# Dilated attention: query blocks without keys behind them taken two in a step, and the forget gates' sums spread through memory instead of by matmuls

## The chip, the cores and the metric

The kernel is one program on one core of a Trainium2 chip. The metric is the device time of one execution in microseconds (us); less is better.

## The reference, cut to what matters

Three transformer blocks follow each other. The change is in the attention of the second one: six heads of dilated attention (three branches, mixed by their softmax sums) and six heads of forgetting attention, 1024 tokens, heads of 64.

```python
def forgetting_attention(q, k, v, log_f):
    c = jnp.cumsum(log_f, axis=1)
    ...
        s = jnp.einsum('bqhd,bkhd->bhqk', qi, k) * scale
        s = s + jnp.transpose(ci, (0, 2, 1))[..., None] - c_k     # c_k: c of every key, for each head
        s = jnp.where(kpos[None, :] <= qpos[:, None], s, -jnp.inf)
        p = jax.nn.softmax(s, axis=-1)
...
DILATION_PAIRS = ((128, 1), (512, 4), (2048, 16))                 # window, dilation
def dilated_branch(q, k, v, window, dilation):
    blk = window // dilation                                      # 128 queries
    ...
    # keys of a query block: its own 128 and the 128 before them (with that dilation), if there are any
    s = jnp.einsum('bnqrhd,bnkrhd->bnrhqk', qs, kc) * (Dh ** -0.5)
    m = jnp.max(s, axis=-1, keepdims=True)
    e = jnp.exp(s - m)
    l = jnp.sum(e, axis=-1)
    num = jnp.einsum('bnrhqk,bnkrhd->bnqrhd', e, vc)
```

## The kernel before, in words

Everything before and after this stage is dense projections and MLPs on TensorE. The stage of interest lies between the last projection of the second block (`ka2`) and the first scores of forgetting attention.

The dilated part is cut into 72 units, `DUN = (branch, pair of heads, query block)`, 24 for each branch. A unit has 128 queries of two heads. `has_prev` says whether there are 128 keys behind its own 128: in branch 0 for 7 of 8 blocks, in branch 1 for 4 of 8, in branch 2 for none. Branches 1 and 2 read the queries and keys with a step of 4 and 8 elements (`dtok`); branch 0 reads them side by side.

Each unit passes through six operations on three engines, staggered over four steps of one loop:

- `dscores` (TensorE, L911): two heads' matmuls into one of two double banks `ps[0]`, `ps[1]`, 128 or 256 keys wide;
- `dmax` (VectorE, L2218): for each head, mask, negate, and keep the minimum, out of PSUM into `pd[n % 3]`;
- `dsoft` (ScalarE, L1544): exp in place with its sum, for each head;
- `dturn` (TensorE, L941), two steps behind the scores: 2 or 4 transposes of 128x128 into one half of `ps[2]`;
- `dcopy` (VectorE L1837, or ScalarE L1535 where `by_act` says so): that half into `qd_[n % 3]`, 256 or 512 columns;
- `dpv` (TensorE, L960), three steps behind: 2 or 4 matmuls with the values into `misc`. `dout` moves `misc` to `NUM` after every fourth unit (L1553 on ScalarE, L1837 on VectorE).

TensorE's order in step s is `dscores(s)`, `dturn(s-2)`, `dpv(s-3)`. VectorE's is `dmax(s)`, `dcopy(s-2)`, `dout(s-3)`; ScalarE's `dsoft(s-1)`, `dcopy(s-2)`, `dout(s-3)`.

Six times in that loop, after units 5, 17, 29, 41, 53 and 65, TensorE also makes `gate_sums(hd)` (L929): a matmul for each 512 columns, of `SEL` (a 6-row selector) with `CF` (the six heads' sums of the forget gates, 6 rows x 1024), which write row `hd` to all 128 partitions of the `ps` bank whose turn it is. ScalarE's `gate_out` (L1558) copies it with scale -1 to `CN[:, hd, :]`. The next user of that bank but one waits for this copy. The first `soft` of forgetting attention on VectorE (L2239) reads `CN`, and its scores (L975) come right behind the last dilated steps.

SyncE issues all DMAs (L2785) in program order: the weights of the next stage, `V4`, `SEL`, then, each behind its branch, the small stores `msc<-ML`, the load of `V16`, and `MN<-msc`.

A float32 matmul shows as two records, so x4 of L911 or x8 of L960 are two and four matmuls.

Of the kernel before, what the change touches and what calls it, by code (L numbers as in the profile page):

```python
# [16 lines left out]
P = 128  # L17
# [190 lines left out]
DSEQ = []  # L208
for _n in range(len(DUN)):
    DSEQ.append(("unit", _n))  # L210
    if _n % 12 == 5:
        DSEQ.append(("gate", _n // 12))

# [32 lines left out]
def build(nc, d, out):  # L246
    ctx = ExitStack()
    with ctx:
# [97 lines left out]
        SEL = at("SEL", RO, [6, 6, P])  # L346
# [50 lines left out]
        msc = nc.dram_tensor("msc", (S, 36), F, kind="Internal").ap()  # L397

# [44 lines left out]
        dnames = (["const", "meta", "mask", "wg", "sgl0", "sgl1", "vs", "sel", "v4", "v16", "b3", "out"]  # L443
# [22 lines left out]
        def dslot(n):  # L466

            return ps[DSEQ.index(("unit", n)) % 2]

# [14 lines left out]
        def by_act(n):  # L484

            br, t_, u = DUN[n]
            return has_prev(br, u) == 1 and u % 3 == 0
# [43 lines left out]
        def tensor(e):  # L531
# [369 lines left out]
            def dscores(n):  # L901

                br, t_, u = DUN[n]
                pv_ = has_prev(br, u)
                w = P * (1 + pv_)
                side_by(("unit", n))
                if n == 0:
                    q.wait_ge(*dv("kb2"))
                for hh in range(2):
                    r_ = slice(64 * hh, 64 * hh + 64)  # L910
                    i = e.matmul(dslot(n)[:, 512 * hh:512 * hh + w], dtok(QB[r_, t_, :], br, u, 0), dtok(KB[r_, t_, :], br, u, pv_), start=True, stop=True)  # L911
                i.then_inc(*pe.inc(f"ds{n}"))

            def side_by(x):

                i = DSEQ.index(x)
                if i > 1:
                    what, m = DSEQ[i - 2]
                    q.wait_ge(*(dv(f"dm{m}") if what == "unit" else ac(f"cn{m}")))
                elif held[i]:  # L920
                    q.wait_ge(*freed(held[i]))
# [10 lines left out]
            def dturn(n):  # L932
                br, t_, u = DUN[n]
                q.wait_ge(*ac(f"dp{n}"))
                if n > 1:
                    q.wait_ge(*at_of(f"dq{n - 2}"))
                elif held[2]:
                    q.wait_ge(*freed(held[2]))
                at_ = 512 * (n % 2)
                for j in range(2 * (1 + has_prev(br, u))):  # L940
                    i = e.transpose(ps[2][:, at_ + P * j:at_ + P * j + P], pd[n % 3][:, blk(j)], ident[:])  # L941
                i.then_inc(*pe.inc(f"dT{n}"))

            def dpv(n):

                br, t_, u = DUN[n]
                nb, g = 1 + has_prev(br, u), n // 8
                q.wait_ge(*at_of(f"dq{n}"))
# [7 lines left out]
                for j in range(nb):  # L956
                    v_ = (VB[:, (u - nb + 1 + j) % 8, :], V4[:, (4 * (u // 4 - nb + 1 + j) + u % 4) % 8, :], V16[:, u, :])[br]
                    for hh in range(2):
                        hd = 2 * t_ + hh
                        i = e.matmul(misc[64 * hh:64 * hh + 64, blk(u)], v_[:, 64 * hd:64 * hd + 64], qd_[n % 3][:, blk(nb * hh + j)], start=(j == 0), stop=(j == nb - 1))  # L960
                i.then_inc(*pe.inc(f"dpv{n}"))
# [18 lines left out]
            n = len(DUN)  # L980
            for s_i in range(n + 4):
                if s_i < n:
                    dscores(s_i)
                    if s_i % 12 == 5:
                        gate_sums(s_i // 12)
# [8 lines left out]
            def fturn(n):  # L994
# [3 lines left out]
                for hh in range(2):  # L998
                    if n:
                        q.wait_ge(*(dv if hh else ac)(f"fq{n - 1}"))  # L1000
                    else:
                        q.wait_ge(*at_of("dq70"))
                        q.wait_ge(*at_of("dq71"))
# [198 lines left out]
        def scalar(e):  # L1202
# [323 lines left out]
            def dcopy(n):  # L1526

                br, t_, u = DUN[n]
                if not by_act(n):
                    return  # L1530
                w = 2 * P * (1 + has_prev(br, u))
                q.wait_ge(*pe(f"dT{n}"))
                if n > 2:
                    q.wait_ge(*pe(f"dpv{n - 3}"))
                e.activation(qd_[n % 3][:, 0:w], ps[2][:, 512 * (n % 2):512 * (n % 2) + w], ACT.Copy).then_inc(*ac.inc(f"dq{n}"))  # L1535

            def dsoft(n):
                br, t_, u = DUN[n]
                w = P * (1 + has_prev(br, u))
                for hh in range(2):  # L1540
                    q.wait_ge(*dv(f"dm{n}" if hh else f"dm{n}a"))
                    p_ = pd[n % 3][:, w * hh:w * hh + w]
                    c_ = 2 * t_ + hh
                    i = e.activation(p_, p_, ACT.Exp, scale=-1.0, bias=ML[:, br, u, c_:c_ + 1], accum_out=ML[:, br, u, 6 + c_:7 + c_])  # L1544
                    i.then_inc(*ac.inc(f"dp{n}" if hh else f"dp{n}a"))

            def dout(n):

                br, t_, u = DUN[n]
                if u != 7:  # L1550
                    return
                q.wait_ge(*pe(f"dpv{n}"))
# [14 lines left out]
            n = len(DUN)  # L1567
            q.wait_ge(*pe("ka2"))
            for s_i in range(n + 4):
# [6 lines left out]
                if s_i < n and s_i % 12 == 6:  # L1576
                    gate_out(s_i // 12)
# [4 lines left out]
            def fcopy(n):  # L1582
# [3 lines left out]
                q.wait_ge(*(pe(f"fpv{n - 3}") if n > 2 else pe("dpv71")))  # L1586
# [240 lines left out]
        def vector(e):  # L1827
# [330 lines left out]
            log_sum("fa", T[1][0:6, :], T[0][0:6, :])  # L2158
# [40 lines left out]
            def dcopy(n):  # L2199
                br, t_, u = DUN[n]  # L2200
                if by_act(n):
                    return
                w = 2 * P * (1 + has_prev(br, u))
                q.wait_ge(*pe(f"dT{n}"))
                if n > 2:
                    q.wait_ge(*pe(f"dpv{n - 3}"))
                copy(qd_[n % 3][:, 0:w], ps[2][:, 512 * (n % 2):512 * (n % 2) + w], f"dq{n}")

            def dmax(n):

                br, t_, u = DUN[n]
                pv_ = has_prev(br, u)
                w = P * (1 + pv_)
                q.wait_ge(*pe(f"ds{n}"))
                q.wait_ge(*(pe(f"dT{n - 3}") if n > 2 else pe("ka2")))
                for hh in range(2):
                    c_ = 2 * t_ + hh
                    e.tensor_tensor_reduce(out=pd[n % 3][:, w * hh:w * hh + w], in0=dslot(n)[:, 512 * hh:512 * hh + w], in1=dmask(br, pv_), scale=-1.0, scalar=3.0e38, op0=ADD, op1=MIN, accum_out=ML[:, br, u, c_:c_ + 1]).then_inc(*dv.inc(f"dm{n}" if hh else f"dm{n}a"))  # L2218

            def dout(n):  # L2220
# [3 lines left out]
                q.wait_ge(*pe(f"dpv{n}"))  # L2224
                copy(dnum(br, t_, 0), v3(misc[:, 0:512], 4), f"nu{n // 8} 0")

            def soft(k, i_):
# [13 lines left out]
            n = len(DUN)  # L2241
# [11 lines left out]
            def fcopy(n):  # L2253
# [3 lines left out]
                q.wait_ge(*(pe(f"fpv{n - 3}") if n > 2 else pe("dpv71")))  # L2257
# [522 lines left out]
        def sync(e):  # L2780
# [324 lines left out]
```

## Time and profile before

| what | value |
|---|---|
| median of 3 runs | 3621.45 us (3615.03 to 3622.73) |
| profiled execution, its own time | 3618.45 us |
| its span, first to last instruction | 3616.3 us |
| TensorE busy (matmul) | 3517.2 us, 97% |
| VectorE, ScalarE busy | 1604.5 us, 1013.1 us |
| chain that ended last | TensorE 91%, VectorE 4%, ScalarE 2% |
| mean granted clock of TensorE | 0.975 |
| first scores L911 to first scores L975 | 1461.78 to 1625.58 us, 163.8 us |

The page gives times of one profiled execution. A view of it in order of time gives the start of a group of instructions, how long it lasted, its engine, line and operands, the number of records, and, in brackets, the idle time of the engine before it with what ended it. TensorE's durations overlap, since matmuls are pipelined: what a group costs there is the distance from its start to the start of the next group, not its duration. PEclk is the clock that TensorE was granted: 1.00 is 2.4 GHz and 0.50 is 1.2 GHz, its two levels; values between them are means of a stretch that has both.

### The profile page before, as it was taken

Reading aid. Unit: us, or ns where it says so; the run is one execution under the profiler, and the core shown is the slowest. Engines: PE = TensorE matmul, PEld = TensorE weight load, DVE = VectorE, ACT = ScalarE, POOL = GpSimd, SP = SyncE. Lnnn points to the kernel's source line nnn. Section 1 sums busy time; section 2 is a strip of 40 time slices with the busy share of each in tenths; the row PEclk is TensorE's granted clock in tenths of the full one; section 3 lists DMA queues with packets and bytes.
Section 4 is the critical chain, followed back from the end, with each engine's and each line's share of the span. In section 5 each row is a group of like instructions: output and inputs, shape, how many; then the busy total and the mean of one; then the engine's idle time right before and its main releaser. Section 6 shows DMA issues by size and latency. Waiting matters only on the chain.

```text
span 3616.3 us, 39495 instructions
## 1 busy us (share of the span) xinstructions
PE 3517.2 (97%) x17066; PEld 2827.0 (78%) x17066; DVE 1604.5 (44%) x1648; ACT 1013.1 (28%) x1458; POOL 1265.9 (35%) x647
## 2 busy tenths in 40 slices
PE   8999999999999999998999999999998999999997
PEld 6887888888888788655688888888887778888886
DVE  4654343333333485445545445444635351222224
ACT  5423221111112411544423222222322333222222
POOL 3113335444444322001223343443534353333333
PEclk9999999999999999969999999999999999999998
DMA  2112212222222211100111232231311121111113
GB/s 107 39 55 81 101 53 88 88 88 88 93 90 79 77 64 47 48 2 3 59 47 54 70 98 63 95 99 62 106 41 35 41 79 50 50 47 50 48 49 119
DMA packets 88569, 239.80 MB, mean 66 GB/s; under 512 B 13238, under 2 KB 20166, under 8 KB 88268
## 3 DMA queue, kind: packets, MB, share of 16 engines
q1 hardware_dynamic: 88396, 237.28, 20.2%
q8 instruction: 134, 2.20, 0.3%
q14 instruction: 39, 0.32, 0.0%
HBM read 219.27 MB, written 17.97 MB: 66 GB/s over the span
## 4 chain that ended last, share of the span: by engine, by line
PE 91%; DVE 4%; ACT 2%; POOL 2%; DMA 1%; issue 0%; SPq 0%; DVEq 0%; ACTq 0%
PE ps L576 27%; PE ps L577 26%; PE ps L579 26%; PE ps L911 2%; PE ps L941 1%; PE ps L960 1%; PE ps L975 1%; POOL wlo L2580 1%; PE ps L746 1%; DVE T L1831 1%; PE ps L1022 1%; PE ps L1006 1%; POOL GL L2586 1%; PE ps L604 0%; PE ps L606 0%; PE ps L1036 0%
## 5 line engine op out<-in xcount | busy, mean ns | idle before, releaser
L2580 POOL TENSOR_TENSOR wlo<-raw,whi 128x1024 fp32r<-128x1024 f32 (+3 forms) x367 | 697.3, 1900 | 1672.0 <-ACT whi L1217 1671.9
L576 PE MATMUL ps<-HH,whi 128*128 128x512 f32 (+2 forms) x2736 | 1084.1, 396 | 21.4 <-POOL wlo L2580 10.0
L577 PE MATMUL ps<-HL,whi 128*128 128x512 f32 (+2 forms) x2736 | 1071.7, 392 | 0.0
L579 PE MATMUL ps<-HH,wlo 128*128 128x512 f32 (+2 forms) x2736 | 848.0, 391 | 0.0
L1217 ACT ACTIVATE whi<-raw 128x1024 fp32r<-128x1024 f32 (+3 forms) x367 | 309.8, 844 | 1657.9 <-PE ps L579 1468.6
L576 PEld LDWEIGHTS ps<-HH,whi 128*128 128x128 f32 (+2 forms) x2736 | 514.8, 188 | 135.3 <-issue 7.2
L576 PE MATMUL ps<-GH,whi 128*128 128x512 f32 x1520 | 598.4, 394 | 3.7 <-POOL GH L2586 2.4
L579 PEld LDWEIGHTS ps<-HH,wlo 128*128 128x128 f32 (+2 forms) x2736 | 513.6, 188 | 112.7 <-issue 0.8
L577 PEld LDWEIGHTS ps<-HL,whi 128*128 128x128 f32 (+2 forms) x2736 | 514.7, 188 | 109.4 <-issue 2.3
L577 PE MATMUL ps<-GL,whi 128*128 128x512 f32 x1520 | 591.7, 389 | 0.0
L579 PE MATMUL ps<-GH,wlo 128*128 128x512 f32 x1520 | 469.9, 390 | 0.0
L1831 DVE TENSOR_TENSOR X<-ps,X 128x1024 f32<-128x1024 f32 (+1 forms) x186 | 225.1, 1211 | 491.3 <-PE ps L579 489.7
L576 PEld LDWEIGHTS ps<-GH,whi 128*128 128x128 f32 x1520 | 286.3, 188 | 63.0 <-issue 3.0
L579 PEld LDWEIGHTS ps<-GH,wlo 128*128 128x128 f32 x1520 | 286.4, 188 | 60.0
L577 PEld LDWEIGHTS ps<-GL,whi 128*128 128x128 f32 x1520 | 285.6, 188 | 57.1
L2586 POOL TENSOR_TENSOR GL<-T,GH 128x1024 fp32r<-128x1024 f32 x86 | 206.9, 2406 | 320.8 <-ACT GH L1427 211.0
L2072 DVE TENSOR_REDUCE adat<-raw 128x128 f32<-128x1024 f32 x92 | 186.4, 2027 | 249.8 <-POOL raw L2586 249.8
L1842 DVE TENSOR_TENSOR T<-ps,RT 128x1024 f32<-128x1024 f32 x72 | 88.2, 1225 | 309.0 <-PE ps L579 277.1
L1831 DVE TENSOR_TENSOR T<-ps,RT 128x1024 f32<-128x1024 f32 (+2 forms) x34 | 41.6, 1223 | 262.9 <-PE ps L579 251.1
L1834 DVE SCALAR_TENSOR_TENSOR T<-T,cols,T 128x1023 f32<-128x1023 f32 x88 | 127.4, 1448 | 62.1 <-ACT T L1658 60.5
L1427 ACT ACTIVATE GH<-T 128x1024 fp32r<-128x1024 f32 x64 | 67.9, 1060 | 258.6 <-DVE T L1831 258.6
L1831 DVE TENSOR_TENSOR T<-T 128x1024 f32<-128x1024 f32 (+3 forms) x74 | 118.7, 1604 | 40.7 <-ACT T L1419 39.6
(363 smaller groups left out, 3124.9 us busy)
## 6 DMA issues: line engine op xcount, KB each, us to landing
raw<-in_w_up SPq DMA_DIRECT2D x76, 512.0 KB, 3.4
raw<-in_w_in SPq DMA_DIRECT2D x70, 512.0 KB, 3.3
raw<-in_w_fc SPq DMA_DIRECT2D x64, 512.0 KB, 3.3
raw<-in_w_down SPq DMA_DIRECT2D x104, 256.0 KB, 2.7
raw<-in_w_ada SPq DMA_DIRECT2D x48, 512.0 KB, 3.5
raw<-in_w_fc SPq DMA_DIRECT2D x64, 256.0 KB, 2.7
X<-in_xT SPq DMA_DIRECT2D x16, 512.0 KB, 7.1
raw<-in_w_out SPq DMA_DIRECT2D x16, 512.0 KB, 3.3
```

The costliest lines, as they stand in the source:

```text
L576: e.matmul(o_[0:m, half(hf)], whi_[:, k, :], hi[k0 + k][:, half(hf)], start=first, stop=False)
L577: e.matmul(o_[0:m, half(hf)], whi_[:, k, :], lo[k0 + k][:, half(hf)], start=False, stop=False)
L579: i = e.matmul(o_[0:m, half(hf)], wlo_[:, k, :], hi[k0 + k][:, half(hf)], start=False, stop=last)
L911: i = e.matmul(dslot(n)[:, 512 * hh:512 * hh + w], dtok(QB[r_, t_, :], br, u, 0), dtok(KB[r_, t_, :], br, u, pv_), start=True, stop=True)
L1217: e.activation(whi_of(name), raw_of(name), ACT.Copy).then_inc(*ac.inc("hi " + name))
L1427: e.activation(GH[:, sl, :], t[:], ACT.Copy).then_inc(*ac.inc(f"{up}hi{f}"))
L1831: e.tensor_tensor(o, a, b, op).then_inc(*dv.inc(*names))
L1834: e.scalar_tensor_tensor(out=o, in0=a, scalar=s_, in1=b, op0=op0, op1=op1).then_inc(*dv.inc(*names))
L1842: e.tensor_tensor(dst, ps[slot[g]][:], RT[:], MUL).then_inc(*dv.inc("free " + g, *names))
L2072: e.tensor_reduce(adat[:, f % 2, :], raw_of(name).rearrange("p (k m) -> p m k", k=8), AX.X, ADD).then_inc(*dv.inc("red " + name))
L2580: e.tensor_tensor(wlo_of(name), raw_of(name), whi_of(name).bitcast(F), SUB).then_inc(*po.inc("lo " + name))
L2586: e.tensor_tensor(o, a, b, op).then_inc(*po.inc(*names))
```

## The change

Units are put into 54 steps, `DSTEP`. Where a unit has no keys behind it in branches 1 and 2, it shares a step with its neighbour: in branch 1 that makes 6 pairs beside 12 single units, in branch 2 12 pairs. Branch 0 stays at one unit in each of its 24 steps. A pair's four score blocks lie in one `ps` bank pair, its four transposes in one half of `ps[2]`, so that such a step has the shape of a step with keys behind. `dmax` and `dsoft` stay one instruction for each head and unit; `dcopy`, the waits and the increments of TensorE and of the copies are one for a step.

`gate_sums`, `gate_out` and `SEL` go. `CF` is now summed with the sign turned; SyncE stores its six rows to memory (`csc`), waits for that, and loads each row back onto all 128 partitions of `CN`, six loads. The first `soft` waits for the last of them.

```diff
-DSEQ = []
-for _n in range(len(DUN)):
-    DSEQ.append(("unit", _n))
-    if _n % 12 == 5:
-        DSEQ.append(("gate", _n // 12))
+DSTEP = []
+for _n, (_br, _t, _u) in enumerate(DUN):
+    if _br == 2 or _br == 1 and _u < 4:
+        if _u % 2 == 0:
+            DSTEP.append((_n, _n + 1))
+    else:
+        DSTEP.append((_n,))
+DLAST = len(DSTEP) - 1
...
+        csc = nc.dram_tensor("csc", (6, S), F, kind="Internal").ap()
...
+        def dcols(s):
+            own = [1 + has_prev(DUN[n][0], DUN[n][2]) for n in DSTEP[s]]
+            return sum(own), [(n, sum(own[:x]), own[x]) for x, n in enumerate(DSTEP[s])]
...
+            def dscores(s):
+                if s > 1:
+                    q.wait_ge(*dv(f"dm{DSTEP[s - 2][-1]}"))
+                elif held[s]:
+                    q.wait_ge(*freed(held[s]))
+                if s == 0:
                     q.wait_ge(*dv("kb2"))
...
+                for n, c0, own in dcols(s)[1]:
+                    br, t_, u = DUN[n]
+                    for hh in range(2):
+                        r_ = slice(64 * hh, 64 * hh + 64)
+                        o0 = 512 * hh + P * c0
+                        i = e.matmul(ps[s % 2][:, o0:o0 + P * own], dtok(QB[r_, t_, :], br, u, 0), dtok(KB[r_, t_, :], br, u, own - 1), start=True, stop=True)
+                i.then_inc(*pe.inc(f"ds{s}"))
...
-            def gate_sums(hd):
-                x = ("gate", hd)
-                side_by(x)
-                q.wait_ge(*dma["sel"]("sel"))
-                q.wait_ge(*dv("cf"))
-                for hf in range(2):
-                    i = e.matmul(ps[DSEQ.index(x) % 2][:, half(hf)], SEL[0:6, hd, :], CF[0:6, half(hf)], start=True, stop=True)
-                i.then_inc(*pe.inc(f"cn{hd}"))
...
+            def dturn(s):
+                q.wait_ge(*ac(f"dp{DSTEP[s][-1]}"))
+                if s > 1:
+                    q.wait_ge(*at_of(f"dq{s - 2}"))
...
+                for j in range(2 * dcols(s)[0]):
+                    i = e.transpose(ps[2][:, at_ + P * j:at_ + P * j + P], pd[s % 3][:, blk(j)], ident[:])
+                i.then_inc(*pe.inc(f"dT{s}"))
...
+            def dsoft(s):
+                nb, units = dcols(s)
+                for n, c0, own in units:
+                    br, t_, u = DUN[n]
+                    for hh in range(2):
+                        q.wait_ge(*dv(f"dm{n}" if hh else f"dm{n}a"))
+                        c_, at_ = 2 * t_ + hh, P * (nb * hh + c0)
+                        p_ = pd[s % 3][:, at_:at_ + P * own]
+                        i = e.activation(p_, p_, ACT.Exp, scale=-1.0, bias=ML[:, br, u, c_:c_ + 1], accum_out=ML[:, br, u, 6 + c_:7 + c_])
...
-            def gate_out(hd):
-                x = ("gate", hd)
-                q.wait_ge(*pe(f"cn{hd}"))
-                e.activation(CN[:, hd, :], ps[DSEQ.index(x) % 2][:], ACT.Copy, scale=-1.0).then_inc(*ac.inc(f"cn{hd}"))
...
-            log_sum("fa", T[1][0:6, :], T[0][0:6, :])
+            q.wait_ge(*ac("fa ln"))
+            q.wait_ge(*dv.now())
+            tt(T[0][0:6, :], T[0][0:6, :], T[1][0:6, :], SUB, "fa log")
...
                 if k == 0:
-                    q.wait_ge(*ac("cn5"))
+                    q.wait_ge(*dma["cn"]("cn 5"))
...
-            q.wait_ge(*dv("ka2"))
-            load("sel", SEL[:], d["sel"], "sel")
+            q.wait_ge(*dv("cf"))
+            load("cs", csc, CF[0:6, :], "cs")
+            q.wait_ge(*pe("ka2"))
+            q.wait_ge(*dma["cs"]("cs"))
+            for hd in range(6):
+                load("cn", CN[:, hd, :], csc[hd].unsqueeze(0).broadcast_to([P, S]), f"cn {hd}")
```

`dpv`, `dmax`, `dcopy` and `dout` are rewritten over steps in the same way.

## Rows read from the trace of the kernel before

**Rows 1.** The page: busy times of the engines, and granted clock in 40 slices.
```profile
PE 3517.2 (97%) x17066; PEld 2827.0 (78%) x17066; DVE 1604.5 (44%) x1648; ACT 1013.1 (28%) x1458; POOL 1265.9 (35%) x647
...
PEclk9999999999999999969999999999999999999998
```
**Rows 2.** In order of time, TensorE: first scores of branches 0, 1, and forgetting attention.
```profile
1461.78 0.49 PE L911 MATMUL ps<-KB,QB 64*128 64x128 f32 x4
...
1509.33 0.83 PE L911 MATMUL ps<-KB,QB 64*128 64x128 f32 x4
...
1625.58 3.79 PE L975 MATMUL ps<-KA,QA 64*128 64x512 f32 x8
...
1632.16 1.77 PE L975 MATMUL ps<-KA,QA 64*128 64x512 f32 x8 [1.51 <-DVE FM L2239]
```
**Rows 3.** In order of time, TensorE, branch 1 at clock 1.00: keys behind.
```profile
1541.81 1.28 PE L911 MATMUL ps<-KB,QB 64*128 64x256 f32 x4
1543.02 0.66 PE L941 MATMUL ps<-ident,T 128*128 128x128 f32 x4
...
1544.19 0.83 PE L911 MATMUL ps<-KB,QB 64*128 64x128 f32 x4
```
**Rows 4.** The same view, branch 2 at clock 1.00: no keys behind.
```profile
1574.40 0.84 PE L911 MATMUL ps<-KB,QB 64*128 64x128 f32 x4
1575.17 0.44 PE L941 MATMUL ps<-ident,T 128*128 128x128 f32 x2
...
1575.91 0.84 PE L911 MATMUL ps<-KB,QB 64*128 64x128 f32 x4
```
**Rows 5.** The same view, branch 1 at clock 0.50, keys behind.
```profile
1522.94 1.28 PE L911 MATMUL ps<-KB,QB 64*128 64x256 f32 x4
1524.15 1.12 PE L941 MATMUL ps<-ident,T 128*128 128x128 f32 x4
1525.19 0.70 PE L960 MATMUL ps<-T,V 128*64 128x128 f32 x4
```
**Rows 6.** The same view: the second gate sum and what waited behind it.
```profile
1492.63 1.98 PE L929 MATMUL ps<-CF,SEL 6*128 6x512 f32 x4
1494.54 0.66 PE L941 MATMUL ps<-ident,T 128*128 128x128 f32 x4
...
1498.98 0.70 PE L911 MATMUL ps<-KB,QB 64*128 64x256 f32 x4 [1.61 <-ACT CN L1558]
```
**Rows 7.** The same view: the third and the fifth of six gate sums.
```profile
1519.57 2.20 PE L929 MATMUL ps<-CF,SEL 6*128 6x512 f32 x4
...
1578.20 2.79 PE L929 MATMUL ps<-CF,SEL 6*128 6x512 f32 x4
```
**Rows 8.** Busy time by stretch: stretch, length, engines' busy times, PEclk, DMA share, GB/s.
```profile
1500.00:1504.00 4.00, 4.00 (x25) 2.35 (x25) 2.58 (x10) 2.18 (x8) 0.00 (x0) 0.59 0.03 6
...
1521.00:1528.00 7.00, 7.00 (x28) 3.40 (x26) 3.67 (x11) 2.75 (x8) 0.00 (x0) 0.51 0.00 0
1528.00:1548.00 20.00, 20.00 (x136) 12.28 (x136) 10.90 (x49) 11.82 (x46) 0.00 (x0) 1.00 0.00 1
1548.00:1569.00 21.00, 18.98 (x89) 10.20 (x89) 8.73 (x32) 8.15 (x28) 0.00 (x0) 0.51 0.01 1
...
1579.00:1630.00 51.00, 48.96 (x211) 24.73 (x209) 20.55 (x96) 19.91 (x80) 0.00 (x0) 0.50 0.03 5
```
**Rows 9.** Groups by line and shape, 1461 to 1626 us: busy, mean ns, idle before.
```profile
L1544 ACT ACTIVATE T<-T,ML 128x128 f32<-128x128 f32 x78 | 30.3, 391 | 19.0 <-DVE ML L2218 18.8
...
L2218 DVE CUSTOM_DVE_ANT_0 T<-ps,negm 128x128 f32<-128x128 f32 x78 | 19.5, 288 | 36.5 <-PE ps L911 36.3
L1837 DVE COPY T<-ps 128x512 f32<-128x512 f32 x24 | 16.5, 688 | 5.9 <-PE ps L941 5.7
...
L1553 ACT ACTIVATE NUM<-ps 128x512 f32<-128x512 f32 x8 | 7.2, 903 | 22.6 <-PE ps L960 22.6
```
**Rows 10.** DMA issues of SyncE: count, KB each, median us to landing.
```profile
X<-xsc SPq DMA_DIRECT2D x8, 512.0 KB, 6.5
```

More of the change, by code:

```diff
@@ L442, in build @@
         names = ("pe_done", "act_done", "dve_done", "pool_done")
-        dnames = (["const", "meta", "mask", "wg", "sgl0", "sgl1", "vs", "sel", "v4", "v16", "b3", "out"]
+        dnames = (["const", "meta", "mask", "wg", "sgl0", "sgl1", "vs", "cs", "cn", "v4", "v16", "b3", "out"]
                   + [f"x{k}" for k in range(8)] + [f"w{k}" for k in range(4)] + [f"sg{k}" for k in range(4)]
@@ L464, in dtok @@
             return ap.rearrange("p (j u) -> p u j", u=8)[:, u, :]
-        def dslot(n):
-            return ps[DSEQ.index(("unit", n)) % 2]
+        def dcols(s):
+            own = [1 + has_prev(DUN[n][0], DUN[n][2]) for n in DSTEP[s]]
+            return sum(own), [(n, sum(own[:x]), own[x]) for x, n in enumerate(DSTEP[s])]
         def dnum(br, t_, hf):
@@ L482, in dmask, with by_act @@
             return negm[:, mk:mk + 1 + pv_, :].rearrange("p a b -> p (a b)")
-        def by_act(n):
-            br, t_, u = DUN[n]
+        def by_act(s):
+            br, t_, u = DUN[DSTEP[s][0]]
             return has_prev(br, u) == 1 and u % 3 == 0
@@ L898, in tensor @@
                     turn_now()
[L901 to L907, printed above, removed]
-                    q.wait_ge(*dv("kb2"))
[L909 to L921, printed above, removed]
-            def gate_sums(hd):
-                x = ("gate", hd)
-                side_by(x)
-                q.wait_ge(*dma["sel"]("sel"))
-                q.wait_ge(*dv("cf"))
-                for hf in range(2):
-                    i = e.matmul(ps[DSEQ.index(x) % 2][:, half(hf)], SEL[0:6, hd, :], CF[0:6, half(hf)], start=True, stop=True)
-                i.then_inc(*pe.inc(f"cn{hd}"))
@@ L937, in dturn @@
+            def dturn(s):
+                q.wait_ge(*ac(f"dp{DSTEP[s][-1]}"))
+                if s > 1:
+                    q.wait_ge(*at_of(f"dq{s - 2}"))
                 elif held[2]:
                     q.wait_ge(*freed(held[2]))
[L939 to L948, printed above, removed]
+                at_ = 512 * (s % 2)
+                for j in range(2 * dcols(s)[0]):
+                    i = e.transpose(ps[2][:, at_ + P * j:at_ + P * j + P], pd[s % 3][:, blk(j)], ident[:])
+                i.then_inc(*pe.inc(f"dT{s}"))
@@ L949, in dpv @@
+            def dpv(s):
+                nb, units = dcols(s)
+                q.wait_ge(*at_of(f"dq{s}"))
+                br, t_, u = DUN[units[0][0]]
+                g = units[0][0] // 8
                 if u % 4 == 0:
@@ L955, in dpv @@
                         q.wait_ge(*(ac("vbT2"), dma["v4"]("v4 1"), dma["v16"]("v16"))[br])
[L956 to L961, printed above, removed]
+                for n, c0, own in units:
+                    u = DUN[n][2]
+                    for j in range(own):
+                        v_ = (VB[:, (u - own + 1 + j) % 8, :], V4[:, (4 * (u // 4 - own + 1 + j) + u % 4) % 8, :], V16[:, u, :])[br]
+                        for hh in range(2):
+                            hd = 2 * t_ + hh
+                            i = e.matmul(misc[64 * hh:64 * hh + 64, blk(u)], v_[:, 64 * hd:64 * hd + 64], qd_[s % 3][:, blk(nb * hh + c0 + j)], start=(j == 0), stop=(j == own - 1))
+                i.then_inc(*pe.inc(f"dpv{s}"))
             def scores(k, i_):
@@ L978, in scores @@
                 i.then_inc(*pe.inc(f"fs{k} {i_}"))
-            n = len(DUN)
+            n = len(DSTEP)
             for s_i in range(n + 4):
@@ L1001, in fturn @@
                     else:
-                        q.wait_ge(*at_of("dq70"))
-                        q.wait_ge(*at_of("dq71"))
+                        q.wait_ge(*at_of(f"dq{DLAST - 1}"))
+                        q.wait_ge(*at_of(f"dq{DLAST}"))
                     for i_ in range(max(j, 4 * qd), 4 * qd + 4):
@@ L1523, in scalar, with dcopy, dout @@
                     turn_now()
-            def dcopy(n):
-                br, t_, u = DUN[n]
-                if not by_act(n):
+            def dcopy(s):
+                if not by_act(s):
                     return
[L1531 to L1547, printed above, removed]
+                w = 2 * P * dcols(s)[0]
+                q.wait_ge(*pe(f"dT{s}"))
+                if s > 2:
+                    q.wait_ge(*pe(f"dpv{s - 3}"))
+                e.activation(qd_[s % 3][:, 0:w], ps[2][:, 512 * (s % 2):512 * (s % 2) + w], ACT.Copy).then_inc(*ac.inc(f"dq{s}"))
+            def dsoft(s):
+                nb, units = dcols(s)
+                for n, c0, own in units:
+                    br, t_, u = DUN[n]
+                    for hh in range(2):
+                        q.wait_ge(*dv(f"dm{n}" if hh else f"dm{n}a"))
+                        c_, at_ = 2 * t_ + hh, P * (nb * hh + c0)
+                        p_ = pd[s % 3][:, at_:at_ + P * own]
+                        i = e.activation(p_, p_, ACT.Exp, scale=-1.0, bias=ML[:, br, u, c_:c_ + 1], accum_out=ML[:, br, u, 6 + c_:7 + c_])
+                        i.then_inc(*ac.inc(f"dp{n}" if hh else f"dp{n}a"))
+            def dout(s):
+                n = DSTEP[s][-1]
                 br, t_, u = DUN[n]
@@ L1551, in dout @@
                     return
-                q.wait_ge(*pe(f"dpv{n}"))
+                q.wait_ge(*pe(f"dpv{s}"))
                 e.activation(dnum(br, t_, 1), v3(misc[:, 512:1024], 4), ACT.Copy).then_inc(*ac.inc(f"nu{n // 8} 1"))
-            def gate_out(hd):
-                x = ("gate", hd)
-                q.wait_ge(*pe(f"cn{hd}"))
-                e.activation(CN[:, hd, :], ps[DSEQ.index(x) % 2][:], ACT.Copy, scale=-1.0).then_inc(*ac.inc(f"cn{hd}"))
             def soft(k, i_):
@@ L1565, in soft @@
                     i.then_inc(*ac.inc(f"fp{k} {i_}" if hh else f"fp{k} {i_}a"))
-            n = len(DUN)
+            n = len(DSTEP)
             q.wait_ge(*pe("ka2"))
@@ L1575, in scalar @@
                     dout(s_i - 3)
-                if s_i < n and s_i % 12 == 6:
-                    gate_out(s_i // 12)
                 if s_i > n:
@@ L1585, in fcopy @@
                 q.wait_ge(*pe(f"fT{n} 0"))
-                q.wait_ge(*(pe(f"fpv{n - 3}") if n > 2 else pe("dpv71")))
+                q.wait_ge(*(pe(f"fpv{n - 3}") if n > 2 else pe(f"dpv{DLAST}")))
                 e.activation(T[n % 3][:, c0:512], ps[2][:, c0:512], ACT.Copy).then_inc(*ac.inc(f"fq{n}"))
@@ L2196, in vector, with dcopy, dmax, dout @@
                     n += 1
-            def dcopy(n):
-                br, t_, u = DUN[n]
-                if by_act(n):
+            def dcopy(s):
+                if by_act(s):
                     return
[L2203 to L2220, printed above, removed]
+                w = 2 * P * dcols(s)[0]
+                q.wait_ge(*pe(f"dT{s}"))
+                if s > 2:
+                    q.wait_ge(*pe(f"dpv{s - 3}"))
+                copy(qd_[s % 3][:, 0:w], ps[2][:, 512 * (s % 2):512 * (s % 2) + w], f"dq{s}")
+            def dmax(s):
+                nb, units = dcols(s)
+                q.wait_ge(*pe(f"ds{s}"))
+                q.wait_ge(*(pe(f"dT{s - 3}") if s > 2 else pe("ka2")))
+                for n, c0, own in units:
+                    br, t_, u = DUN[n]
+                    for hh in range(2):
+                        c_, at_ = 2 * t_ + hh, P * (nb * hh + c0)
+                        e.tensor_tensor_reduce(out=pd[s % 3][:, at_:at_ + P * own], in0=ps[s % 2][:, 512 * hh + P * c0:512 * hh + P * (c0 + own)], in1=dmask(br, own - 1), scale=-1.0, scalar=3.0e38, op0=ADD, op1=MIN, accum_out=ML[:, br, u, c_:c_ + 1]).then_inc(*dv.inc(f"dm{n}" if hh else f"dm{n}a"))
+            def dout(s):
+                n = DSTEP[s][-1]
                 br, t_, u = DUN[n]
@@ L2223, in dout @@
                     return
-                q.wait_ge(*pe(f"dpv{n}"))
+                q.wait_ge(*pe(f"dpv{s}"))
                 copy(dnum(br, t_, 0), v3(misc[:, 0:512], 4), f"nu{n // 8} 0")
@@ L2232, in soft @@
                 if k == 0:
-                    q.wait_ge(*ac("cn5"))
+                    q.wait_ge(*dma["cn"]("cn 5"))
                 elif k == 1:
-                    q.wait_ge(*pe("dpv71"))
+                    q.wait_ge(*pe(f"dpv{DLAST}"))
                 else:
@@ L2239, in soft @@
                     e.tensor_tensor_reduce(out=PF[i_, hh], in0=ps[hh][:, 0:w], in1=CN[:, 2 * t_ + hh, 0:w], scale=-1.0, scalar=3.0e38, op0=ADD, op1=MIN, accum_out=FM[:, k % 2, i_ % 4, hh:hh + 1]).then_inc(*dv.inc(f"fm{k} {i_}" if hh else f"fm{k} {i_}a"))
-            n = len(DUN)
+            n = len(DSTEP)
             for s_i in range(n + 4):
@@ L2256, in fcopy @@
                 q.wait_ge(*pe(f"fT{n} 1"))
-                q.wait_ge(*(pe(f"fpv{n - 3}") if n > 2 else pe("dpv71")))
+                q.wait_ge(*(pe(f"fpv{n - 3}") if n > 2 else pe(f"dpv{DLAST}")))
                 copy(T[n % 3][:, 512 + c0:1024], ps[2][:, 512 + c0:1024], f"fq{n}")
```

8 lines of the change are left out of this document (removed).

## The prediction

> **What bounds the kernel now.** I read the page first. TensorE is busy for 97% of the span and no other engine for more than 44% [rows 1], so outside this stage nothing is to be had, and the change touches nothing there. The clock line has one low digit, slice 19, about 1627 to 1718 us [rows 1]; slices are coarse, so I then read the stage in order of time and by stretches. From the first scores of branch 0 at 1461.78 us, over those of branch 1 at 1509.33, to those of forgetting attention at 1625.58 [rows 2], it takes 47.5 + 116.3 us. TensorE has hardly a wait in it: its steps follow each other at fixed distances, which depend on the shape and on the clock alone. So the stage is a sum of TensorE groups in program order, and the reader can add them.
>
> At clock 1.00, a step of branch 1 with keys behind takes 1541.81 to 1544.19: 1.21 us for the scores, 1.17 for four transposes and four value matmuls, 2.38 together [rows 3]. A step with no keys behind takes 1574.40 to 1575.91, 1.51 us, of which 0.77 are scores [rows 4]. A gate sum takes 1492.63 to 1494.54, 1.91 us, and later the bank's next user stands 1.61 us behind ScalarE's copy [rows 6].
>
> The clock is the other half. It is at 1.2 GHz for most of 1521 to 1528, 1548 to 1569 and 1579 to 1630, and at 2.4 GHz in 1528 to 1548 [rows 8]. At 1.2 GHz four transposes take 1524.15 to 1525.19, 1.04 us, while the 256 strided score columns take 1.21 as at full clock [rows 3, 5]. What TensorE did before each fall: gate sums 3 and 5 began 1.4 and 0.8 us before 1521 and 1579 [rows 7, 8], the fourth lies likewise before 1548, and the cold part of 1500 to 1504 follows the 1.61 us wait behind the second [rows 6, 8]. All four falls stand behind a gate sum. The clock came back at 1528 and 1569, both among steps with keys behind; among the small steps of branch 2 it never did in 51 us [rows 8].
>
> **Stretch A, branch 0.** Its 24 steps are untouched. Gone are two gate sums, 2 x 1.91 = 3.8 us, and the 1.6 us wait [rows 6]. Gone with its cause is the cold part of 1500 to 1504: a mean of 0.59 over 4 us is 3.3 us at 1.2 GHz [rows 8]; with transposes at 1.04 against half of 1.17 [rows 3, 5] it gives back about 1.3. Sum 6.7.
>
> **Stretch B, branches 1 and 2.** The trace has no pair, but a step with keys behind has its shape: four blocks of scores, four transposes, four value matmuls. Transposes and value matmuls are taken from it at 1.17. The pair's scores load weights four times, not twice. Low end: the extra blocks cost only their columns, as between one block (0.77) and two (1.21), that is 0.44, so 1.21 [rows 3, 4]. High end: nothing overlaps, 2 x 0.77 = 1.54. I take 1.21, because a transpose too has a new weight load for 128 columns, and four of them cost no more than 0.6 us. At 2.4 GHz the new stretch is 30 scores x 1.21 = 36.3, plus 31 x 1.17 = 36.3 (the last transposes and value matmuls ahead of forgetting attention count once more), 72.6 us in place of 116.3. Gain 43.7. In it are the four other gate sums, the waits for their copies, 18 times the saving of a pair over two single steps (2 x 1.51 - 2.38 = 0.64, 11.5 us), and, the largest part, the clock.
>
> The Trainium skill, page TensorE: Matmul & The Clock Gate, Part 3, says that a weight load overlaps a running matmul only where their row groups differ; the second unit of a pair loads into the same row groups. By that rule the sum would stand at the high end, 6 us more. The rows of the transposes, all in the same row groups, speak against it.
>
> **What covers it.** In a pair VectorE has four reductions (19.5 us / 78 = 0.25 busy each) and one copy of 512 columns, 0.69: 1.7 us; ScalarE four exps of 0.39 and a quarter of a NUM copy of 0.90: 1.8 [rows 9]. Both stay under 2.38, and VectorE's own NUM copy, once in four steps, is caught up in the next. Where the cover is thinnest, in the one step of four with ScalarE's NUM copy, it is 4 x 0.39 + 0.90 = 2.46 against 2.38; if the slack of the steps around it didn't take that up, it would cost 0.1 us each time, under 1 us in all. Exps, copies and reductions in total are as before; six copies of 1024 columns leave ScalarE.
>
> **The memory detour.** The store of 24 KB and six loads of 512 KB stand on SyncE behind V4. Behind its two waits are queued the small stores of `ML` and the load of V16; both already wait for branch 0 to end, 47 us later, so nothing late arises. A load of 512 KB lands in 6.5 us [rows 10]; one after the other that is 39 us from about 1467, while the first reader comes after 110 us. Cost nothing. If that cover were gone, VectorE's first `soft` would wait, and TensorE's second scores behind it. The turned sign is one VectorE operation for one.
>
> **Stretch C, forgetting attention.** Its first scores run at 1.2 GHz in 3.79 us, the second at full clock in 1.77 [rows 2]; entered warm, 2.0 us are gained. Then TensorE waits for VectorE (1.51 us before the second scores, [rows 2]), and the clock may fall there as before, so I count no more. Bounds: 0 to 5.
>
> **Sum.** 6.7 + 43.7 + 2.0 = 52.4 us. The profiled execution took 3618.45 us, 2.15 more than its span; less 52.4 is 3566. The median of the runs is 3.0 above it; the same from there is 3569. I forecast 3568.
>
> **The rivals.**
>
> *The clock stays low in the pairs.* For it: in branch 2 it stayed low for 51 us with no long wait in sight, and a fall can come from anything. Against: at 1.2 GHz it came back both times in steps of the pairs' shape, and held from 1528 to 1548 [rows 8]. All of branches 1 and 2 at 1.2 GHz would be 36.3 + 31 x 2.08 = 100.8 us, 28 more, and C's 2 are lost: 3598. The Trainium skill, same page, Part 4, says that transposes don't count as activity for the clock, and a pair is by instructions a third transposes; by that rule this rival is what one would expect. In between lie single cold stretches: a step is then 3.29 against 2.38, so 20 us of them cost 5.5. Chance of all: 0.05; of a part of 6 us or more: 0.13.
>
> *Pairs don't do what they say.* TensorE's instructions are as many as before, and if a pair costs two single steps, 18 x 0.64 = 11.5 us don't come: 3580. Against: distances between groups hold a fixed part (four transposes against two). If only the scores fail to overlap (1.54), it is 18 x 0.33 = 6: 3574. Chance 0.10 for both.
>
> *CN comes late, slower than before.* Each load reads one row of 4 KB 128 times. If those reads served one another in turn, a load could take many times 6.5 us. `soft` would begin at about 1577 (1461.8 + 40.8 + 72.6, and 1.8 of scores), so the gain is gone when the last lands after 1629, that is from 27 us a load on; at 30 us a load it lands at 1647, 70 late: 3638. Speaks for it: no row has a store followed by such a load of it. Against: it is four times the dearest 512 KB load [rows 10]. Chance 0.02.
>
> **How the numbers follow.** Forecast 3568 with 0.70: 3560 to 3575, by C's end and the high end of the scores. The range reaches down to 3557 (C's 5 us and some waits that go) and up to 3590, to most of the partly cold cases; it leaves out full cold and late CN. A measurement tells 0.2%, 7 us, from no change. Faster 0.96: forecast and the first two rivals, even at 3598. Same 0.015, slower 0.025: late CN and a rest.
>
> **What would show it.** Steps of 2.4 us from the first pair of branch 1 on, clock 1.00 from 1461 to the first scores of forgetting attention, these at about 1575 with 1.8 us instead of 3.8, no L929 and L1558, the last load of CN landed before 1510. Wrong in B's size if pair scores take 1.5; wrong in the clock if PEclk falls in a stretch without a gate sum; wrong in the cover if TensorE waits for VectorE or ScalarE before L911 or L941. A VectorE wait for CN would make the rest void.

## The result and the profile after

The changed kernel takes 3571.2 us, median of four runs (3567.95 to 3576.02), against 3621.3 for the kernel before; the ratio is 0.9864, 95% interval 0.9852 to 0.9876. The gain is 50.1 us; the sum had said 52.4, the forecast time was 3568.

The profiled execution took 3576.0 us, the slowest of the four. Its page, busy times and granted clock, answers to [rows 1]:

```profile
PE 3478.9 (97%) x17042; PEld 2820.8 (79%) x17042; DVE 1598.3 (45%) x1630; ACT 1005.4 (28%) x1452; POOL 1266.5 (35%) x647
...
PEclk9999999999999999999999999999999999999998
```

The low digit of the clock line is gone. It stood in the 18th of the 40 slices, 1537 to 1627 us, which is the second half of the stage; the prediction had called it slice 19, 1627 to 1718. The stage by its three branches (stretch, length, busy times of TensorE, its weight loads, VectorE, ScalarE and GpSimd, granted clock, DMA share, GB/s), to be held against [rows 8]:

```profile
1465.00:1506.00 41.00, 39.16 (x339) 24.36 (x337) 29.37 (x117) 30.00 (x102) 2.35 (x1) 1.00 0.35 130
1506.00:1549.00 43.00, 43.00 (x316) 27.65 (x313) 26.90 (x115) 26.42 (x103) 0.00 (x0) 1.00 0.12 39
1549.00:1580.00 31.00, 30.83 (x260) 23.54 (x258) 20.87 (x112) 23.11 (x104) 0.00 (x0) 1.00 0.03 3
```

PEclk is 1.00 from the first scores of the stage to the first of forgetting attention. TensorE in order of time, the boundaries of [rows 2] and pairs of branches 1 and 2 (L918 scores, L929 transposes, L951 value matmuls, L965 scores of forgetting attention):

```profile
1465.91 0.49 PE L918 MATMUL ps<-KB,QB 64*128 64x128 f32 x4
...
1506.17 1.30 PE L918 MATMUL ps<-KB,QB 64*128 64x128 f32 x8
1507.41 0.66 PE L929 MATMUL ps<-ident,T 128*128 128x128 f32 x4
1507.99 0.66 PE L951 MATMUL ps<-T,VB 128*64 128x128 f32 x8
1508.58 1.30 PE L918 MATMUL ps<-KB,QB 64*128 64x128 f32 x8
...
1554.07 1.32 PE L918 MATMUL ps<-KB,QB 64*128 64x128 f32 x8
1555.32 0.66 PE L929 MATMUL ps<-ident,T 128*128 128x128 f32 x4
...
1579.75 1.99 PE L965 MATMUL ps<-KA,QA 64*128 64x512 f32 x8
...
1584.42 1.77 PE L965 MATMUL ps<-KA,QA 64*128 64x512 f32 x8 [1.44 <-DVE FM L2223]
```

From start to start: a pair's scores take 1.24 us in branch 1 and 1.25 in branch 2, its step 2.41 and 2.42. The stage takes 1465.91 to 1579.75, 113.8 us for 163.8. All that TensorE waited for in it, by the view of waits (who waited for whom, us in total, times, longest) from 1470 us on, is

```profile
PE ps L929 <- ACT T L1532: 0.2, 1, 0.2
```

Starts of these groups give a table that the experiments use. "Ahead" is up to the first dilated scores; "forgetting" from its first scores to the first matmul of the output projection; "rest" from there to the end of the span. The last column is how much of the dilated stage stands at 1.2 GHz. The column of medians is of all runs of a kernel, the others of its one profiled execution. Ratios below are against the kernel before as it ran beside each (median 3624.0 for e0 to e3, 3620.8 for e4 to e7).

| kernel | median us | ahead | dilated stage | forgetting | rest | of the stage at 1.2 GHz |
|---|---|---|---|---|---|---|
| before | 3621.3 | 1461.8 | 163.8 | 142.9 | 1847.8 | 77 |
| changed | 3571.2 | 1465.9 | 113.8 | 141.6 | 1852.5 | 0 |
| e0, changed again | 3570.9 | 1461.5 | 113.8 | 138.8 | 1850.9 | 0 |
| e1, no gate sums, no pairs | 3579.3 | 1464.3 | 125.1 | 138.8 | 1850.9 | 0 |
| e2, pairs with gate sums | 3588.8 | 1463.0 | 134.9 | 141.4 | 1847.6 | 24 |
| e3, before, gate sums of 128 rows | 3602.7 | 1463.5 | 150.0 | 142.0 | 1846.7 | 28 |
| e4, as e3, two units later | 3589.6 | 1462.1 | 137.8 | 139.0 | 1847.2 | 0 |
| e6, before, two units later | 3612.0 | 1466.0 | 152.8 | 142.1 | 1846.6 | 52 |
| e7, changed, CN loaded late | 3570.8 | 1465.6 | 113.8 | 141.6 | 1849.1 | 0 |
| e5, changed, operands in order | 3549.8 | 1465.8 | 97.4 | 139.0 | 1846.1 | 0 |

### The profile page after: what moved, and what is told of

Its sections match the earlier page's. It is cut to its first block, busy times and chain, and to the rows that moved or that the text cites. A ratio compares the mean times of both kernels' runs of the same rounds, so it can differ in the third digit from the quotient of the medians.

```text
span 3573.9 us, 39428 instructions
## 1 busy us (share of the span) xinstructions
PE 3478.9 (97%) x17042; PEld 2820.8 (79%) x17042; DVE 1598.3 (45%) x1630; ACT 1005.4 (28%) x1452; POOL 1266.5 (35%) x647
## 4 chain that ended last, share of the span: by engine, by line
PE 91%; DVE 4%; ACT 2%; POOL 2%; DMA 1%; issue 0%; SPq 0%; DVEq 0%; ACTq 0%
PE ps L580 27%; PE ps L581 26%; PE ps L583 26%; PE ps L918 1%; POOL wlo L2564 1%; PE ps L929 1%; PE ps L951 1%; PE ps L965 1%; PE ps L750 1%; PE ps L994 1%; DVE T L1813 1%; PE ps L1010 1%; PE ps L608 1%; PE ps L610 1%; PE ps L609 1%; POOL GL L2570 1%
```

## The experiments

My theory: the gain is mostly the clock's. It falls behind gate sums, and the small steps of branch 2 can't raise it again; the pairs save their fixed part beside it. The rivals: the small steps bring it down by themselves, so that the pairs are what cures it; or once down it stays down in pairs too. A small step is one with a single unit that has no keys behind: two score matmuls, two transposes, two value matmuls, 1.51 us at 2.4 GHz [rows 4].

### e0: the changed kernel again

No edit.

> The changed kernel once more, to see which of its parts repeat. My reading: the dilated stage repeats at 113.8 us with no stretch at 1.2 GHz in it, and the cold stretches before and behind the stage (1202 us, 1680 to 1731 us) move or change length from one execution to the next, so that they explain the 5 us between 3576.0 and 3571.2. Rival: the four short cold stretches at 1680 to 1731 us in forgetting attention are a lasting price of the change and stand here again. Total 3571 either way.

Measured: 3570.9 us, ratio to the kernel before 0.9854 (0.9839 to 0.9869). The dilated stage is 113.8 us again at clock 1.00. Outside it the three stretches differ by 1.6 to 4.5 us between the two profiles of one kernel. The changed kernel had four short stretches at 1.2 GHz from 1680 to 1731 us, around the end of forgetting attention, of 3.4 us each. Here there are three, from 1705 to 1726, of 3.4, 6.8 and 3.4 us: 13.7 us in both. The kernel before has two such, 1760.1 to 1773.8 and 1777.2 to 1780.6, 17.1 us, so they are no price of the change. Microseconds outside the stage can't be laid to the change one by one, and a profile's span is read by stage.

### e1: sums through memory, no pairs

```diff
-for _n, (_br, _t, _u) in enumerate(DUN):
-    if _br == 2 or _br == 1 and _u < 4:
...
+DSTEP = [(_n,) for _n in range(len(DUN))]
```

> One part alone: the sums through memory, all 72 units in steps of their own, no pairs. Theory: the clock falls only behind gate sums, so it stays at 2.4 GHz. Stage: 40.8 (branch 0) + 12 x 2.38 + 12 x 1.51 (branch 1) + 24 x 1.51 (branch 2) + 1 = 125 us, against 163.8 before and 113.8 with pairs; total 3582. Rival: the small steps of branch 2 are too light by themselves; the clock falls there, steps of 2.02, 12 us more: 3594 and PEclk near 0.5 in the last third of the stage.

Measured: 3579.3 us (ratio 0.9876, 0.9859 to 0.9892), stage 125.1. Branches 1 and 2, same columns as above:

```profile
1505.00:1552.00 47.00, 47.00 (x317) 28.11 (x315) 27.60 (x120) 27.10 (x104) 0.00 (x0) 1.00 0.11 36
1552.00:1589.00 37.00, 37.00 (x256) 23.60 (x254) 22.81 (x122) 23.42 (x99) 0.00 (x0) 1.00 0.02 2
```

TensorE in order of time, one step of branch 2 and the next one's scores:

```profile
1576.48 0.84 PE L912 MATMUL ps<-KB,QB 64*128 64x128 f32 x4
1577.26 0.44 PE L923 MATMUL ps<-ident,T 128*128 128x128 f32 x2
1577.62 0.44 PE L945 MATMUL ps<-T,V 128*64 128x128 f32 x4
1577.99 0.84 PE L912 MATMUL ps<-KB,QB 64*128 64x128 f32 x4
```

The small steps hold 2.4 GHz for all 37 us of branch 2. The first rival falls. Taking out the gate sums alone takes 38.7 us off the stage (163.8 less 125.1); the pairs add 11.3 (125.1 less 113.8), where the prediction had 11.5 (18 pairs x 0.64).

### e2: pairs, with gate sums as before

```diff
+                    if s_i in GATE_AT:
+                        gate_sums(GATE_AT[s_i])
...
+                if s_i - 1 in GATE_AT:
+                    gate_out(GATE_AT[s_i - 1])
...
-            for hd in range(6):
-                load("cn", CN[:, hd, :], csc[hd].unsqueeze(0).broadcast_to([P, S]), f"cn {hd}")
+            load("sel", SEL[:], d["sel"], "sel")
```

> The other part alone: pairs as in the changed kernel, but the six gate sums by matmuls with ScalarE's copies, as before. Theory: each gate sum costs 1.9 to 2.7 us and 0 to 2 us of wait (about 18 us in all), the clock falls behind about four of them, and comes back within about 7 us because the pairs are as dense as steps with keys behind; with 28 us at 1.2 GHz, where a step takes 3.29 for 2.38, that is 8 us. Stage 113.8 + 18 + 8 = 140, total 3597. Rival (density alone sets the clock, gate sums don't): no cold stretch, stage 132, total 3589. A second rival: once fallen it stays low also in pairs: stage 155 or more, total 3612.

Measured: 3588.8 us (0.9902, 0.9887 to 0.9917), stage 134.9. Branch 2 around its first gate sum (L943; L925 scores, L954 transposes, L976 values):

```profile
1565.32 2.28 PE L943 MATMUL ps<-CF,SEL 6*128 6x512 f32 x4
1567.53 1.12 PE L954 MATMUL ps<-ident,T 128*128 128x128 f32 x4
1568.57 1.12 PE L976 MATMUL ps<-T,V 128*64 128x128 f32 x8
1569.62 1.33 PE L925 MATMUL ps<-KB,QB 64*128 64x128 f32 x8
...
1576.55 1.32 PE L925 MATMUL ps<-KB,QB 64*128 64x128 f32 x8
1577.81 0.66 PE L954 MATMUL ps<-ident,T 128*128 128x128 f32 x4
```

Transposes at 1.04 us from 1567.53 on and at 0.58 from 1577.81 on: the clock fell at the gate sum and came back 10 us later, among nothing but pairs. In [rows 7, 8] the same gate sum was followed by 51 us of low clock; so the second rival is refuted. Five of six gate sums were followed by such a fall, of 3.4 to 10.2 us; the second only behind a wait of 1.61 us, the other four without a wait. I had expected 28 us at 1.2 GHz and stage 140; it was 24 us and 134.9, and the sums and waits cost less than the 18 us that I had put on them, by estimate 14 to 15 (21.1 us over the changed stage, less 6 to 7 for 24 us of steps of 3.3 us in place of 2.4).

So each part alone gives more than half of the gain in the stage: 38.7 us (e1) and 28.9 (e2), where both together give 50.0 and not 67.6. What they share is the clock, which either part cures for the most part.

### e3: gate sums that read 128 rows

```diff
-        SEL = at("SEL", RO, [6, 6, P])
+        SEL = at("SEL", RO, [P, 6, P])
...
+            e.memset(CF[:], 0.0).then_inc(*dv.inc("cf0"))
...
-                    i = e.matmul(ps[DSEQ.index(x) % 2][:, half(hf)], SEL[0:6, hd, :], CF[0:6, half(hf)], start=True, stop=True)
+                    i = e.matmul(ps[DSEQ.index(x) % 2][:, half(hf)], SEL[0:P, hd, :], CF[0:P, half(hf)], start=True, stop=True)
```

> The kernel before with one edit: the gate sums' matmuls read 128 rows (122 of them zero) in place of 6, same columns, same result, same copies and waits. If it is the few rows that make TensorE count as little used during a gate sum, the falls behind them go, the small steps stay at 2.4 GHz (if they can hold it), and the stage is 125 + 6 x 1.9 + 6 of waits = 142: total 3600. If it is the wait behind the copy or the break in the order that brings the clock down, nothing changes: 3621, cold stretches at the same places.

Measured: 3602.7 us (0.9944, 0.9929 to 0.9959), stage 150.0: neither 142 nor 164. Three falls were left. The fifth gate sum (L937), and the sixth and what followed:

```profile
1576.20 1.98 PE L937 MATMUL ps<-CF,SEL 128*128 128x512 f32 x4
1578.02 0.38 PE L948 MATMUL ps<-ident,T 128*128 128x128 f32 x2
1578.33 0.44 PE L970 MATMUL ps<-T,V 128*64 128x128 f32 x4
...
1596.12 1.98 PE L937 MATMUL ps<-CF,SEL 128*128 128x512 f32 x4
...
1599.76 0.44 PE L970 MATMUL ps<-T,V 128*64 128x128 f32 x4
1602.23 0.84 PE L919 MATMUL ps<-KB,QB 64*128 64x128 f32 x4 [2.03 <-ACT CN L1569]
1603.01 0.69 PE L948 MATMUL ps<-ident,T 128*128 128x128 f32 x2
```

Each of the three falls came right behind such a wait of TensorE for the copy to CN: 2.27, 2.68 and 2.47 us from the start of the last group to that of the scores, of which 1.61, 2.02 and 2.03 idle. The gate sums without it no longer brought the clock down: among them the third and the fifth, behind which it had fallen in the kernel before [rows 7, 8]. So there seemed to be two causes: the few rows and the wait. The wait is ScalarE's: at the second, fourth and sixth gate sum its copy to `CN` stands right behind its copy to `NUM`, at the others not. The kernel before has the same three waits, that of [rows 6] and these, both while the clock was low already:

```profile
1555.67 0.61 PE L911 MATMUL ps<-KB,QB 64*128 64x128 f32 x2 [2.02 <-ACT CN L1558]
...
1614.24 0.85 PE L911 MATMUL ps<-KB,QB 64*128 64x128 f32 x4 [2.04 <-ACT CN L1558]
```

### e4 and e6: the gate sums two units later, with 128 rows and with 6

```diff
-GATE_AT = {next(_s for _s, _u in enumerate(DSTEP) if 12 * _h + 5 in _u): _h for _h in range(6)}
+GATE_AT = {next(_s for _s, _u in enumerate(DSTEP) if 12 * _h + 7 in _u): _h for _h in range(6)}
```

> The kernel before with gate sums of 128 rows (as in e3) and each of the six two units later, so that ScalarE's copy to CN no longer stands right behind its copy of NUM. Theory with two causes (few rows in the gate sum; the long wait of 2.3 to 2.7 us from the last group to the next scores, in e3 before each of its three falls): both are gone, so the stage runs at 2.4 GHz from end to end, 125.1 as without gate sums + 6 x 2.0 for sums and short waits = 137, total 3590. Rival: gate sums bring the clock down by breaking the order of steps, whatever their shape: falls stay, stage 150, total 3603.

> The kernel before with the six gate sums two units later, 6 rows as before. Same theory: the falls behind a long wait go, those behind the few rows stay, and in branch 2 the small steps don't bring the clock back: stage 150 to 162, total 3608 to 3620, cold stretches starting at a gate sum. Rival: the wait was the only cause that counts and the rows of e3 helped by being shorter: stage 138, total 3591.

Measured, e4: 3589.6 us (0.9921, 0.9904 to 0.9938), stage 137.8. Its three branches:

```profile
1462.00:1509.00 47.00, 44.14 (x361) 26.88 (x360) 30.64 (x121) 33.24 (x109) 3.03 (x2) 1.00 0.13 47
1509.00:1556.00 47.00, 45.99 (x290) 26.79 (x290) 24.74 (x110) 26.68 (x99) 0.00 (x0) 1.00 0.10 35
1556.00:1600.00 44.00, 44.00 (x288) 27.16 (x288) 25.93 (x130) 27.43 (x109) 0.00 (x0) 1.00 0.02 2
```

Six gate sums, no fall in the stage. Two waits for the copy to CN are left, of 1.01 us each, and the clock stays up behind them too.

Measured, e6: 3612.0 us (0.9977, 0.9967 to 0.9988), stage 152.8. Branch 2 (from 1566 us, with the last step of branch 1 ahead of it), in two stretches, before and behind the fall in it:

```profile
1563.00:1580.00 17.00, 17.00 (x115) 10.66 (x114) 10.34 (x46) 10.01 (x42) 0.00 (x0) 0.98 0.04 4
1581.00:1619.00 38.00, 38.00 (x176) 20.37 (x178) 17.50 (x84) 17.08 (x68) 0.00 (x0) 0.50 0.00 1
```

TensorE in order of time at the first gate sum of branch 2:

```profile
1577.72 0.84 PE L919 MATMUL ps<-KB,QB 64*128 64x128 f32 x4
1578.50 1.98 PE L937 MATMUL ps<-CF,SEL 6*128 6x512 f32 x4
1580.41 0.49 PE L948 MATMUL ps<-ident,T 128*128 128x128 f32 x2
1580.83 0.70 PE L970 MATMUL ps<-T,V 128*64 128x128 f32 x4
```

TensorE has no wait before that fall, only a gate sum of 6 rows, and the small steps behind it stay at 1.2 GHz to the end. With 128 rows in the same place (e4) there is none. Two shorter falls, at 1529.5 and 1556.8 us, 6.8 us each, stand behind the third and the fourth gate sum, without a wait before them either. Each cause was taken away alone (e3 the few rows, e6 the long wait) and both together (e4): 77 us at 1.2 GHz in the stage with both, 28 with the wait alone, 52 with the few rows alone, 0 with neither. So both are real. Two limits: in branch 0 no gate sum of 6 rows brought the clock down without a long wait (the first in the kernel before, in e2 and e6, the second in e6), and why is open; and every long wait of these runs' stages stands behind a gate sum. In forgetting attention, which has none, waits of 1.44, 1.62 and 1.94 us stand ahead of the fall at 1594.9 us in the changed kernel.

### e7: CN loaded late

```diff
-            for hd in range(6):
-                load("cn", CN[:, hd, :], csc[hd].unsqueeze(0).broadcast_to([P, S]), f"cn {hd}")
...
                 elif br == 1:
...
+                    for hd in range(6):
+                        load("cn", CN[:, hd, :], csc[hd].unsqueeze(0).broadcast_to([P, S]), f"cn {hd}")
```

> The changed kernel, its six loads of CN issued behind branch 1 (at about 1550 in place of 1473 us), beside the small stores. My reading: they need under 15 us to land and the first reader comes at 1582, so nothing changes: 3571, stage 113.8, forgetting attention 139 to 142. Rival (the detour is near its limit, or its traffic costs TensorE something): VectorE's first reduction of forgetting attention waits for CN, or steps in branch 2 grow beyond 2.43 us; 5 us or more.

Measured: 3570.8 us (0.9862, 0.9846 to 0.9878), stage 113.8. The loads were issued from 1550.7 to 1554.2 us and landed in 5.5 to 9.1 us, before the first reader at 1581.7; in the changed kernel from 1473.4 to 1476.0, in 3.9 to 7.7 us. The detour has 98 us of room in the changed kernel, from the last landing to the first reader, and is free even with 18 (e7).

### e5: operands of branches 1 and 2 in order

```diff
+            for t_ in range(3):
+                q.wait_ge(*pe(f"ds{8 * t_ + 7}"))
+                for x, (src, dst) in enumerate(((QB, PQ), (KB, PK))):
...
+                    e.tensor_copy(dst[t_][:].rearrange("p (r j) -> p r j", r=4), src[:, t_, :].rearrange("p (j r) -> p r j", r=4)).then_inc(*po.inc(f"far {t_}" if x else f"farq {t_}"))
```

> The changed kernel with one addition: GpSimd, idle in this stage, puts Q and K of each pair of heads into the order of branch 1 while branch 0 still runs (six copies of 128x1024), so that branch 1 reads side by side and branch 2 with a step of 2 in place of 8. Theory: the score groups cost 1.21 to 1.25 because of the step of their operands, whatever the clock; side by side four blocks cost 0.64 as in branch 0, steps of branch 1 take 1.81 in place of 2.40 unless VectorE or ScalarE bind (both have 1.8 us of work a pair): 18 x 0.58 = 10 us in branch 1, 0 to 7 in branch 2; total 3555 to 3562. Rival: the score groups' price is that of four matmuls with float32 weights, not of the reading: no gain, 3571; or the other engines bind at once: gain under 4.

The score matmuls of branches 1 and 2 then read `PQ` and `PK` in place of `QB` and `KB`.

Measured: 3549.8 us (3548.7 to 3551.1; ratio to before 0.9808, 0.9793 to 0.9822). Pairs of branch 1, and of branch 2 (L931 scores, L942 transposes):

```profile
1506.08 0.71 PE L931 MATMUL ps<-PK,PQ 64*128 64x128 f32 x8
1506.73 0.66 PE L942 MATMUL ps<-ident,T 128*128 128x128 f32 x4
...
1542.38 0.74 PE L931 MATMUL ps<-PK,PQ 64*128 64x128 f32 x8
1543.06 0.66 PE L942 MATMUL ps<-ident,T 128*128 128x128 f32 x4
```

Scores of a pair take 0.65 us in place of 1.24, and 0.68 with a step of 2 in place of 1.25. The step is 1.82 us in branch 1 and 1.85 in branch 2, about what VectorE and ScalarE have to do by the prediction's sum (1.7 and 1.8), and in branch 2 TensorE now waits for ScalarE once, for 0.8 us. The stage is 97.4 us, 16.4 less: 10.4 in branch 1 and 6.0 in branch 2, as expected. The total is 21.0 less than e7, which ran beside it; the 4.6 that are left lie outside the stage, which is as much as the stretches there move between two profiles of one kernel (e0), and they take the total out of the 3555 to 3562 that I had expected. GpSimd's six copies take 2.1 us each; five run beside branch 0 and the sixth beside the first pairs of branch 1. This version beats both kernels.

## Why the prediction was right

**What bounds the stage.** TensorE's groups in program order, with two prices for two clocks. e1 is the sharpest test: 125 us from start-to-start distances, 125.1 measured. The changed stage is 113.8 us where stretches A and B had made it 113.4.

**Stretch A.** 1465.91 to 1506.17 is 40.3 us; 47.5 less 6.7 had been 40.8.

**Stretch B.** 73.6 us (1506.17 to 1579.75) against 72.6. The term of the pair's scores, 1.21 us, was the low end of its range and measured 1.24 and 1.25; that is 0.6 us in 18 pairs, and most of the rest is one late group at the end. The bound from "nothing overlaps", 1.54, was far off. The Trainium skill, page TensorE: Matmul & The Clock Gate, Part 3, says that a weight load overlaps a running matmul only where their row groups differ; in this trace the second unit's loads, into the same rows as the first unit's, added at most 0.03 to 0.04 us to a pair's scores.

**The clock.** The step that carried the largest part of the gain held: no gate sum, no fall in the stage. The argument had read it off the coincidence of four falls and four gate sums; e3, e4 and e6 made causes of it, and corrected the reading in one point: the wait behind the copy is a cause beside the few rows (e3), and a gate sum of 6 rows is one without a wait (e6). The rival's line that branch 2 stayed low "with no long wait in sight" is right for the fall at 1579.2 us, but a wait of 2.04 us stands behind the sixth gate sum, at 1612. In e2 pairs raised the clock from 1.2 GHz within 10 us. The Trainium skill, same page, Part 4, says that transposes don't count as activity for the clock, from which the prediction made a rival; a third of a pair's matmuls are transposes, and the other two thirds were enough in e2, so the rival is refuted while no run here tells whether transposes count.

**The part that the clock has in it.** The prediction put 11.5 us on the pairs' fixed part, 11.3 were measured. It called the clock the largest part of the gain in B, without a number. The stages of before, e4, e1 and the changed kernel, 163.8, 137.8, 125.1 and 113.8 us, split the 50.0 us: 26.0 for the clock with the long waits, 12.7 for the gate sums with the two short waits beside them, 11.3 for the pairs. TensorE waited 5.8 us for the copies to CN in the kernel before and 2.0 in e4, so the clock by itself is about 22 us, by this estimate: the largest part, but under half of the gain in the stage, and less than my theory had it. The prediction was silent on one thing: with the gate sums gone the small steps would have held 2.4 GHz by themselves, so that pairs are worth 11 us there and 29 us beside gate sums. It had the small steps' 51 us at low clock as a sign for a rival; they only show that such steps don't raise a clock once it is down.

**Stretch C.** 1579.75 to 1584.42 is 4.67 us for 6.58 [rows 2], 1.9 for the 2.0 that were counted. Forgetting attention as a whole gained 1.3 in the first profile and 4.1 in e0, within 0 to 5.

**Cover and detour.** TensorE waited 0.2 us in the stage from 1470 us on; CN landed by 1484, 98 us early.

**The sum.** 50.1 measured of 52.4 by the medians of the first comparison, 53.1 by those of the second (3624.0 and 3570.9). The difference is of the size of what moves outside the stage. The two profiled executions of the first comparison differ by only 42.4 us (3618.45 and 3576.02): 50.0 gained in the stage and 1.3 in forgetting attention, less 4.1 and 4.7 that the stretches ahead and behind were longer, which the change doesn't touch. So the stage came out as summed (50.0 for 50.4), and that the medians agree to 2 us is in part luck.

## What to carry to other kernels

Where TensorE is the bound and its groups follow one another without waits, read the distances from start to start at each clock and add them; that gave this stage within 1%. Look then at what stands right before each fall of the granted clock. Here one gate sum on 6 rows was followed by 51 us at 1.2 GHz, because the small steps behind it didn't raise the clock again; at 0.5 us lost in each of them that is some 12 us, by estimate. Giving the steps the shape of a pair (e2) cured most of it, and taking the triggers away (e1, e4) all of it. And when a group costs the same at both clocks, it is not the array that sets its price: here it was the step of its operands, and an idle engine could put them in order.

## What the runs showed of the hardware that was not expected

- Small steps (1.51 us) held 2.4 GHz for 37 us (e1), and the same steps stayed at 1.2 GHz for 38 us in e6, where they take 2.03. The state depends on what went before.
- A gate sum of 128 rows left the clock alone where one of 6 rows with the same columns brought it down (the third to the fifth in e4 and e6).
- A wait of 1.6 to 2.0 us behind a gate sum of 128 rows brought the clock down three times of three (e3); two waits of 1.01 us didn't (e4).
- The score group of four blocks costs 1.21 to 1.26 us with operands 4 or 8 float32 apart, at either clock (the changed kernel, e2); at 2.4 GHz it costs 0.65 with them side by side and 0.68 two apart (e5).
